# One level of Strassen's scheme for the key products of a paged attention loop

## The chip, the cores and the metric

The kernel runs on one NeuronCore of a Trainium2 chip. The metric is the device time of one execution in microseconds (us). TensorE (PE) multiplies; VectorE (DVE), ScalarE (ACT) and GpSimd (POOL) work element by element; SyncE (SP) issues nearly all DMAs. The engines run their own instruction lists in order and wait for each other on semaphores only.

## The reference

One step of a hybrid decoder layer for 256 prompt tokens and for 8 sequences ("batches" below) of 4 new tokens each. An mLSTM branch and an MLA attention branch are gated and added, then comes a convolutional feed-forward part. The change lies in the MLA attention of the 8 sequences, each of which has 1024 cached positions in 8 pages of 128 rows. A cached row is a latent of 512 numbers and a rotary key of 64:

```python
def mla_keys(c_kv, k_rope, w_uk, g_kn, g_kr):
    k_nope = jnp.einsum('...sc,chd->...shd', c_kv, w_uk)
    k_r = jnp.broadcast_to(k_rope[..., None, :], k_nope.shape[:-1] + (B_ROPE,))
    return qk_norm(k_nope, k_r, g_kn, g_kr)
def mla_attend(q, k, c_kv, mask, w_uv):
    s = jnp.einsum('bqhe,bkhe->bhqk', q, k).astype(jnp.float32) * ATTN_SCALE
    s = jnp.where(mask, s, -jnp.inf)
    p = jax.nn.softmax(s, axis=-1).astype(c_kv.dtype)
    o_lat = jnp.einsum('bhqk,bkc->bqhc', p, c_kv)
    return jnp.einsum('bqhc,chv->bqhv', o_lat, w_uv)
```

The 16 keys of 128 numbers of a cached row are needed only for their norm (qk_norm divides each key by its root mean square). The scores themselves can be had from the latent, with a query that was multiplied by w_uk beforehand.

## The kernel before

All work is in stages with barriers between them: projections and prompt attention, then the **page loop** (this change), then the mLSTM heads, branch projections, the output projection and the feed-forward part. Weights pass in tiles of 2048 columns through four staging slots (`stage`); a weight or activation is split into a high and a low part of type fp32r, and a product is made of three matmuls (high by high, high by low, low by high). `split_hi` (L281, ScalarE) and `split_lo` (L288, VectorE) split weight tiles; `block` (L300, L301, L305) multiplies one by the 288 tokens, in 48 matmuls.

**Page loop.** `batches` unrolls batches 0, 1, 6 and 7 and loops over 2 to 5, two at a time. For each page `page_load` brings the latent and rotary rows in 32 by 32 blocks, VectorE transposes them (`turn`, L1806), ScalarE rounds them to the high part (`hi`, L1707), VectorE makes the low part (`lo`, L1810). `keys` then multiplies the page (512 features in 4 chunks) by w_uk, kept in SBUF for the whole loop as `ukH` and `ukL`, in five column groups of 448, 384, 384, 384 and 512 columns, a PSUM bank each. The first group carries the 64 multiplied query columns of the batch beside three heads, so that scores come with the keys, and two small matmuls add the rotary part. ScalarE squares each group out of PSUM (`squares`, L1720), and VectorE sums the squares per head (`sums`, L1817). After eight pages `scale` turns the sums into factors on the scores. The softmax and the product with the latents (`maxima`, `spread`, `less`, `exps`, `total`, `denominators`, `values`, `turn_out`, `out`, `out_turned`) of a batch run between the pages of the next one; the latents as values are loaded a second time, untransposed (`latf`, L1488). GpSimd has nothing in this loop.

**Around it.** The stage before loads w_uk again in its last third (`uk_again`), into the four staging slots; at the loop's start four splits turn them into `ukH` and `ukL`. With that the slots are free, and SP fills them with half of w_uv and the first two weight tiles of the next stage. `ukH` and `ukL` lie where xnH and xnL (the split normed activations) lay; these are reloaded from a DRAM copy when the last key product is done (L1529, L1530). After the loop TensorE does the values of the last batch, one block of the next stage, the products with w_uv, a second block, and the stage ends.

Of the kernel before, what the change touches and what calls it, by code (L numbers as in the profile page):

```python
# [25 lines left out]
P = 128  # L26
# [144 lines left out]
def build(nc, A, O):  # L171
# [33 lines left out]
    with ctx:  # L205
# [111 lines left out]
        qlat = sb(kept, "qlat", [P, LC, NB, 2, BH, S_S], F32R)  # L317
        krr2 = sb(kept, "krr2", [P, 3, 2, ROPE])
        krr = krr2[:, :, 0, :]
        rk_new = sb(kept, "rk_new", [P, BH])  # L320
        cnH = sb(kept, "cnH", [P, LC, P], F32R)
        cnH_at = nc.sbuf_base - 4 * LC * P
        cnL = sb(kept, "cnL", [P, LC, P], F32R)
        RAW, QD = 4, P // 4
        RC = P + QD
        raw = sb(kept, "raw", [P, RAW, 4 * RC])
        raw_in = [lasting(f"raw_in{s}") for s in range(RAW)]
# [19 lines left out]
        uk_land = [lasting(f"uk_land{g}") for g in range(4)]  # L347
# [86 lines left out]
        with ExitStack() as heads:  # L434
# [39 lines left out]
            cqH, cqL = (qlat[:].rearrange("p k b o h s -> p (k b o h s)")[:, i * LC * T:(i + 1) * LC * T].rearrange("p (k t) -> p k t", k=LC) for i in range(2))  # L474
# [10 lines left out]
            def B2(name):  # L485
# [24 lines left out]
            r_t, r_sq, r_sum, r_ss, ct_t, ct_ev, cn_z = (  # L510
                sem("kr_" + x) for x in ("t", "sq", "sum", "ss", "ctt", "ctev", "cnz"))
            k_mm, k_sq, k_smp, k_sum, k_add, k_rt, k_rc, k_new, k_nadd, k_nrt = (
                sem("k_" + x) for x in ("mm", "sq", "smp", "sum", "add", "rt", "rc", "new", "nadd", "nrt"))
            u_t, u_ev, u_q, u_ab, u_abt, u_h, u_l = (sem("uk_" + x) for x in ("t", "ev", "q", "ab", "abt", "h", "l"))
# [20 lines left out]
            with nc.Block() as blk:  # L535
                @blk.sync
                def _(sp):
# [69 lines left out]
                    def uk_again(g):  # L607
                        read(VCH + g)
                        for x in range(4):
                            sp.dma_start(chunk_of(VCH + g, 512)[quadrant(x)], uk_q[x][:, :, g * 512:(g + 1) * 512]).then_inc(uk_land[g], 16)  # L610
# [4 lines left out]
                    uk_again(0)  # L615
                    uk_again(1)
# [3 lines left out]
                    for p in range(PAIRS):  # L620
                        out(p)
                        if p == 2:
                            uk_again(2)
                        if p == 4:
                            uk_again(3)

                @blk.tensor
                def _(pe):
# [147 lines left out]
                    def absorbed(j):  # L776
                        pe.wait_ge(u_ab, j + 1)
                        need(pe, u_l, LC * j)
# [124 lines left out]
                    def values(h):  # L903
                        pe.wait_ge(e_tev, h + 1)
                        pe.wait_ge(v_ev, 2 * (h // 4) + 2)
                        if h == 0:
                            pe.wait_ge(u_l, 4 * LC)
# [28 lines left out]
                def _(act):  # L936
# [120 lines left out]
                    def high_part(j):  # L1057
                        act.wait_ge(u_abt, j + 1)
                        for k in range(LC):
                            q_ = bank[7][:, k * P:(k + 1) * P].rearrange("p (g b s) -> p b g s", g=4, b=NB)  # L1060
                            act.activation(qlat[:, k, :, 0, 4 * j:4 * j + 4, :], q_, ACT.Copy).then_inc(u_h, 1)
# [112 lines left out]
                def _(dve):  # L1174
# [3 lines left out]
                    dve.memset(cnH[:].bitcast(F32), 0.0).then_inc(cn_z, 1)  # L1178
                    dve.memset(cnL[:].bitcast(F32), 0.0).then_inc(cn_z, 1)
# [112 lines left out]
                    def low_part(j):  # L1292
                        for k in range(LC):
                            q_ = bank[7][:, k * P:(k + 1) * P].rearrange("p (g b s) -> p b g s", g=4, b=NB)
                            dve.wait_ge(u_h, LC * (j + 1))
                            dve.tensor_tensor(qlat[:, k, :, 1, 4 * j:4 * j + 4, :], q_, qlat[:, k, :, 0, 4 * j:4 * j + 4, :].bitcast(F32),
                                              ALU.subtract).then_inc(u_l, 1)
                    for h in range(BH + 3):
# [16 lines left out]
                        if h >= 10 and (h - 10) % 4 == 0:  # L1315
                            low_part((h - 10) // 4)
# [31 lines left out]
                    low_part(3)  # L1348
# [21 lines left out]
        with ExitStack() as ph:  # L1370
            NJ = NPG + 1
            HQ = BH * S_S
            HALF = NPG // 2
            GC = 512
            UC = BH * NOPE + 2 * HQ
            GROUPS = [(0, 3), (3, 6), (6, 9), (9, 12), (12, 16)]
            KG = len(GROUPS)
            ukH = arena("ukH", [P, LC, UC], 0, F32R)
            ukL = arena("ukL", [P, LC, UC], 4 * LC * UC, F32R)

            def uk_col(h):

                return h * NOPE + (HQ if h < GROUPS[0][1] else 2 * HQ)

            def moving(g, s):

                h0, h1 = GROUPS[g]
                if g:
                    return uk_col(h0), uk_col(h0) + (h1 - h0) * NOPE
                return (0, h1 * NOPE + HQ) if s == 0 else (HQ, h1 * NOPE + 2 * HQ)  # L1390

            def slot(s):

                return slice(0, HQ) if s == 0 else slice(HQ + GROUPS[0][1] * NOPE, 2 * HQ + GROUPS[0][1] * NOPE)

            def parts(s):

                w = GROUPS[0][1] * NOPE
                return (slice(0, HQ), slice(HQ, HQ + w)) if s == 0 else (slice(w, w + HQ), slice(0, w))

            def key_bank(g):
                return bank[g if g < 4 else 5]

            sq = sb(ph, "sq_n", [P, 2, GC])
            mxp = sb(ph, "mxp", [P, 2, P])
            mxw = sb(ph, "mxw", [HQ, 2, P])
            sqr = sb(ph, "sqr_n", [P, 2, ROPE])
            scn = sb(ph, "scn", [N_S, NB, BH, S_S])
            latf = sb(ph, "latf", [P, 2, NPG, KVL + ROPE])
            latT = sb(ph, "latT", [P, KVL + P])  # L1410
            latH = sb(ph, "latH", [P, 2, KVL + P], F32R)
            latL = sb(ph, "latL", [P, 2, KVL], F32R)
# [4 lines left out]
            psums = sb(ph, "psums", [P, 2, HQ])  # L1417
# [1563 lines left out]
```

## Time and profile before

| | us |
|---|---|
| median of 3 runs (2891.14 to 2893.79) | 2893.04 |
| the profiled execution | 2892.51 |
| its span, first to last instruction | 2890.6 |
| TensorE busy | 2838.0 |
| VectorE busy | 1495.8 |
| ScalarE busy | 1131.8 |
| GpSimd busy | 104.6 |

The span is the time between the first and the last instruction, and the profiled execution's time is what the device took for it as a whole. "Busy" counts time in which an instruction of the engine runs; TensorE's matmuls overlap, so its busy time is no measure of how fast they follow each other.

### The profile page before, as it was taken

The page shows a single profiled execution, that of the slowest core. Times are in us where ns is not written, and L with a number is a line of the kernel's source. Part 1 is how long each engine was busy: PE and PEld are TensorE (multiplying, and loading weights), DVE is VectorE, ACT ScalarE, POOL GpSimd, SP SyncE. Part 2 cuts the span into 40 slices and gives each one's busy share as a digit, 9 for nine tenths or more (in the row PEclk, how much of TensorE's full clock was granted, in tenths as well). Part 3 has the DMA queues.
Part 4 walks back from the last instruction along what each step waited for, and adds up shares of the span by engine and source line. Part 5 has one row for each costly group of instructions (what it writes and reads, how often), then busy time and mean ns, then how long its engine had stood idle before and what let it go on. Part 6 is the DMA issues. An engine that isn't in the chain of part 4 may idle for free. (4 is left out here: it accounts for less than half of the span.)

```text
span 2890.6 us, 50971 instructions
## 1 busy us (share of the span) xinstructions
PE 2838.0 (98%) x19086; PEld 2657.2 (92%) x19086; DVE 1495.8 (52%) x2297; ACT 1131.8 (39%) x1813; POOL 104.6 (4%) x346
## 2 busy tenths in 40 slices
PE   8998999999999998999999999999999999999999
PEld 7865898898898887999999999999999999999999
DVE  5465544444444433445454434445677754677644
ACT  5536332332333232444544333333444433444433
POOL 0100000000000000000000000002100000001000
PEclk9999999999999998999999999999999999999999
DMA  6624412112212204656666555556555556555564
GB/s 196 224 77 104 132 44 58 51 37 62 58 35 53 59 31 165 188 176 191 180 195 181 161 170 165 160 171 189 163 162 160 155 157 183 168 166 161 147 176 130
DMA packets 695531, 393.32 MB, mean 136 GB/s; under 512 B 65096, under 2 KB 675986, under 8 KB 694424
## 3 DMA queue, kind: packets, MB, share of 16 engines
q1 hardware_dynamic: 683160, 378.64, 44.9%
q10 hardware_dynamic: 11824, 11.50, 1.2%
q8 instruction: 110, 1.80, 0.3%
q0 software_dynamic: 368, 0.81, 0.1%
q14 instruction: 69, 0.57, 0.1%
HBM read 368.13 MB, written 22.75 MB: 135 GB/s over the span
## 5 line engine op out<-in xcount | busy, mean ns | idle before, releaser
L288 DVE TENSOR_TENSOR w_lo_b<-stage,w_hi_b 128x2048 fp32r<-128x2048 f32 (+1 forms) x289 | 619.0, 2142 | 411.0 <-ACT w_hi_b L281 410.8
L300 PE MATMUL bank<-xnH,w_hi_b 128*128 128x288 f32 x2784 | 756.8, 299 | 3.5 <-PEq L191 3.5
L301 PE MATMUL bank<-xnL,w_hi_b 128*128 128x288 f32 x2784 | 751.4, 297 | 0.0
L281 ACT ACTIVATE w_hi_b<-stage 128x2048 fp32r<-128x2048 f32 (+1 forms) x289 | 517.8, 1792 | 568.2 <-PE bank L305 535.4
L300 PEld LDWEIGHTS bank<-xnH,w_hi_b 128*128 128x128 f32 x2784 | 524.8, 188 | 13.4 <-issue 12.8
L301 PEld LDWEIGHTS bank<-xnL,w_hi_b 128*128 128x128 f32 x2784 | 524.4, 188 | 0.3
L1556 PE MATMUL bank<-ukH,latH 128*128 128x384 f32 (+2 forms) x1280 | 458.0, 358 | 5.0 <-DVE latL L1810 3.9
L1560 PE MATMUL bank<-ukL,latH 128*128 128x384 f32 (+2 forms) x1280 | 459.7, 359 | 0.0
L1561 PE MATMUL bank<-ukH,latL 128*128 128x384 f32 (+2 forms) x1280 | 454.0, 355 | 0.0
L305 PE MATMUL bank<-xnH,w_lo_b 128*128 128x288 f32 x2784 | 396.4, 295 | 0.0
L1817 DVE TENSOR_REDUCE rk<-sq_n 128x3 f32<-128x384 f32 (+1 forms) x320 | 182.1, 574 | 403.3 <-ACT sq_n L1720 403.3
L305 PEld LDWEIGHTS bank<-xnH,w_lo_b 128*128 128x128 f32 x2784 | 378.1, 188 | 0.0
L1720 ACT ACTIVATE sq_n<-bank 128x384 f32<-128x384 f32 (+1 forms) x320 | 163.4, 511 | 437.8 <-PE bank L1561 414.2
L300 PE MATMUL bank<-haH,w_hi_b 128*128 128x288 f32 x1024 | 277.3, 298 | 6.8 <-PEq L191 3.8
L301 PE MATMUL bank<-haL,w_hi_b 128*128 128x288 f32 x1024 | 275.9, 296 | 0.0
L1556 PEld LDWEIGHTS bank<-ukH,latH 128*128 128x128 f32 x1280 | 241.2, 188 | 31.5 <-issue 12.0
L1561 PEld LDWEIGHTS bank<-ukH,latL 128*128 128x128 f32 x1280 | 241.3, 189 | 14.4
L1560 PEld LDWEIGHTS bank<-ukL,latH 128*128 128x128 f32 x1280 | 241.2, 188 | 14.1 <-issue 1.0
L300 PEld LDWEIGHTS bank<-haH,w_hi_b 128*128 128x128 f32 x1024 | 193.4, 189 | 7.5 <-issue 7.3
L301 PEld LDWEIGHTS bank<-haL,w_hi_b 128*128 128x128 f32 x1024 | 194.3, 190 | 0.0
L305 PE MATMUL bank<-haH,w_lo_b 128*128 128x288 f32 x1024 | 151.9, 295 | 0.0
L305 PEld LDWEIGHTS bank<-haH,w_lo_b 128*128 128x128 f32 x1024 | 141.6, 188 | 0.0
(480 smaller groups left out, 2757.1 us busy)
## 6 DMA issues: line engine op xcount, KB each, us to landing
stage<-in_w_in_dram SPq DMA_DIRECT2D x88, 1024.0 KB, 5.2
stage<-in_w_up_dram SPq DMA_DIRECT2D x88, 1024.0 KB, 5.4
stage<-in_w_down_dram SPq DMA_DIRECT2D x64, 704.0 KB, 4.6
raw<-in_cache_kv_latent_dram SPq DMA_DIRECT2D x256, 64.0 KB, 1.8
latf<-in_cache_kv_latent_dram SPq DMA_DIRECT2D x64, 256.0 KB, 2.5
stage<-in_w_branch_a_dram SPq DMA_DIRECT2D x16, 1024.0 KB, 5.5
stage<-in_w_branch_b_dram SPq DMA_DIRECT2D x16, 1024.0 KB, 5.3
stage<-in_w_out_dram SPq DMA_DIRECT2D x16, 1024.0 KB, 5.6
```

The source lines that it names most:

```text
L281: act.activation(h, a, ACT.Copy).then_inc(w_hi, 1)
L288: dve.tensor_tensor(lo, a, h.bitcast(F32), ALU.subtract).then_inc(w_lo, 1)
L300: pe.matmul(out, hi, xH(k), start=first and k == 0, stop=False)
L301: pe.matmul(out, hi, xL(k), start=False, stop=False)
L305: mm = pe.matmul(out, lo, xH(k), start=False, stop=last and k == kc - 1)
L1556: pe.matmul(out, h, ukH[:, k, cols], start=k == 0, stop=False)
L1560: pe.matmul(out, h, ukL[:, k, cols], start=False, stop=False)
L1561: mm = pe.matmul(out, lo, ukH[:, k, cols], start=False, stop=k == LC - 1)
L1720: act.activation(sq[:, (j + g) % 2, 0:(h1 - h0) * NOPE], part, ACT.Square).then_inc(n_sq, 1)
L1817: dve.tensor_reduce(rk[:, b.mod(2), j, h0:h1], sq[:, (j + g) % 2, 0:(h1 - h0) * NOPE].rearrange("p (h d) -> p h d", d=NOPE), AX.X, ALU.add ...
```

## The change

The pages are taken in pairs. With the features in halves 1 and 2 and the heads in halves 1 and 2, the keys of a pair are a product of two matrices of two by two blocks, A (pages by features) and B (features by heads). It is made with seven block products instead of eight (Winograd's form of Strassen's scheme):

- sums on the page side: S1 = A21 + A22, S2 = S1 - A11, S3 = A11 - A21, S4 = A12 - S2, per pair, on GpSimd; the seven operands A11, A12, S2, S3, S1, S4, A22 are split into high part (ScalarE, `split`) and low part (GpSimd, `low`)
- differences on the weight side: T1 to T4, once at the start; the seven operands B11, B21, T2, T3, T1, B22, T4 are split and stay in SBUF, also where the staging slots were
- the products p1 to p7 add up in PSUM as far as the scheme allows; ScalarE copies three partial sums out (`copy_s1`, `copy_u2`, `copy_u4`), VectorE makes three of the four results from a bank and such a copy (`sum11`, `sum22`, `sum21`), and the fourth is squared out of PSUM

Each half of the heads (8 heads) is cut into column groups of 2, 3 and 3 heads, which are 288, 384 and 384 columns wide; the first carries 32 query columns. So a pair has three groups G, twelve a batch, of seven products, and a product is two feature chunks by three matmuls, 42 matmuls a group. The products of a group are interleaved with two of the group before (p3 and p4):

```diff
-                        for j in range(NPG):
-                            keys(b, j)
+                        for G in range(NG):
+                            i, pos = G // 3, G % 3
+                            p1(b, G)
+                            p2(b, G)
+                            if pos == 0:
+                                ropes(b, i)
+                            if not early(b, G - 1):
+                                p3(b, G - 1)
+                            p6(b, G)
+                            p7(b, G)
+                            if not early(b, G - 1):
+                                p4(b, G - 1)
...
+                            p5(b, G)
```

One product, and two with their waits:

```diff
+                        for c in range(2):
+                            hi, lo = (lat[:, a, part, c * P:(c + 1) * P] for part in range(2))
+                            pe.matmul(out, hi, moving(g, op, 0, c, s), start=first and c == 0, stop=False, skip_group_check=not first)
+                            pe.matmul(out, hi, moving(g, op, 1, c, s), start=False, stop=False, skip_group_check=not first)
+                            mm = pe.matmul(out, lo, moving(g, op, 0, c, s), start=False, stop=c == 1, skip_group_check=not first)
+                        mm.then_inc(sem_, 1)
...
+                    def p6(b, G):
+                        pe.wait_ge(e_s1, upto(b, G))
+                        product(b, G, bA[G % 2], S2, T2, k_p[6], False)
...
+                    def p5(b, G):
+                        pe.wait_ge(e_u2, upto(b, G))
+                        product(b, G, bA[G % 2], S1, T1, k_p[5], False)
```

GpSimd per pair, and the order of ScalarE and VectorE in a group (without the parts for starts and ends):

```diff
+                        out, x, y, how = ((latents(S1), a21, a22, ALU.add), (latents(S2), latents(S1), a11, ALU.subtract),
+                                          (a21, a11, a21, ALU.subtract), (latents(S4), a12, latents(S2), ALU.subtract))[n]
+                        pool.tensor_tensor(out, x, y, how).then_inc(f_sum4, 1)
...
+                        pool.wait_ge(a_hi, b.of(7 * PR, 7 * i + op + 1))
+                        need(pool, a_lo, b.of(7 * PR, 7 * i + op))
+                        pool.tensor_tensor(lat[:, op, 1, :], latents(op), lat[:, op, 0, :].bitcast(F32), ALU.subtract).then_inc(a_lo, 1)
...
+                                copy_u4(b, G - 1)
+                                square(b, G - 2, C21, e_c21, e_q21)
+                                split(b, i, S1)
+                            copy_s1(b, G)
+                                split(b, i + 1, A11)
+                                square(b, G - 1, C22, e_c22, e_q22)
+                                split(b, i + 1, A12)
+                            square(b, G, C11, e_c11, e_q11)
+                                square12(b, G - 1)
+                                split(b, i, S4)
+                            copy_u2(b, G)
+                                split(b, i + 1, S2)
+                                split(b, i + 1, S3)
+                                rope_squares(b, i)
+                                    split(b, i, A22)
+                                rope_high(b, i + 1)
+                            if post and G == 2:
+                                root(b - 1)
+                            if post and G == 6:
+                                exps(b - 1)
...
+                                sum22(b, G - 1)
+                                turn(b, i + 1)
+                                norm_sum(b, G - 2, C21, 1, 0, e_q21, e_r21)
+                            sum11(b, G)
+                                norm_sum(b, G - 1, C22, 1, 1, e_q22, e_r22)
+                            norm_sum(b, G, C11, 0, 0, e_q11, e_r11)
+                                norm_sum(b, G - 1, C12, 0, 1, e_q12, e_r12)
+                                sum21(b, G - 1)
```

`turn` transposes both pages of the next pair into one buffer once a pair, when all low parts of the pair before are made. Rotary scores get four small matmuls a pair (`ropes`). The query columns of a batch are also combined and split into seven operands (`query_sums`, `query_low` on GpSimd, `query_high` on ScalarE). The softmax steps of the batch before are spread over the groups; `values` runs in groups 8 and 9, from a buffer of four pages (`value_rows`, waiting for the values' matmuls), the rotary rows have a load of their own. The scores of the new tokens are made of plain fp32 matmuls instead of split ones, and the split of the multiplied queries in the stage before is gone.

Start: `uk_again` loads w_uk by column groups into `stage`. T1 to T4 of the first and third of the groups in memory order are made by VectorE (`uk_sums`), those of the other by GpSimd; `uk_high` (ScalarE) and `uk_low` (VectorE) split the 21 operands, those of the first column group before the first product and the others in groups 0 and 1 of batch 0.

End: xnH and most of xnL are reloaded when p4 of the last pair's first group is done; the slots, the last piece of xnL and w_uv follow in this order, and the next stage's block moves ahead of the values, the second block ahead of the w_uv products:

```diff
+                    sp.wait_ge(k_p[4], upto(b, NG - 3))
+                    sp.dma_start(xnH[:].bitcast(F32), xnH_dram).then_inc(xn_back, 16)
+                    sp.dma_start(xnL[:, 0:KC - 1].bitcast(F32), xnL_dram[:, 0:KC - 1]).then_inc(xn_back, 16)
+                    sp.wait_ge(k_p[4], upto(b, NG - 2))
+                    head_load(sp, At(0), 0)
+                    uv_load(0)
                     for j in range(2, 4):
                         uv_load(j)
-                    sp.wait_ge(n_k, KG * NPG * NB)
-                    sp.dma_start(xnH[:].bitcast(F32), xnH_dram).then_inc(xn_back, 16)
-                    sp.dma_start(xnL[:].bitcast(F32), xnL_dram).then_inc(xn_back, 16)
+                    head_load(sp, At(0), 1)
+                    sp.wait_ge(k_p[4], upto(b, NG - 1))
+                    sp.dma_start(xnL[:, KC - 1:].bitcast(F32), xnL_dram[:, KC - 1:]).then_inc(xn_back, 16)
+                    uv_load(1)
                     sp.wait_ge(f_uv, 4)
```

## Rows read from the trace of the kernel before

**Rows 1.** The page, part 1: busy time, share of the span, instructions.

```profile
PE 2838.0 (98%) x19086; PEld 2657.2 (92%) x19086; DVE 1495.8 (52%) x2297; ACT 1131.8 (39%) x1813; POOL 104.6 (4%) x346
```

**Rows 2.** Stretches: start:end, length, busy time of each engine, granted clock, DMA share.

```profile
284.00:295.00 11.00, 5.71 (x19) 4.14 (x19) 6.60 (x17) 4.44 (x8) 0.00 (x0) 0.76 0.58 149
295.00:1102.00 807.00, 805.91 (x4230) 723.12 (x4230) 356.84 (x694) 259.00 (x619) 0.00 (x0) 1.00 0.21 55
1102.00:1141.00 39.00, 27.19 (x265) 20.72 (x264) 13.22 (x26) 10.26 (x14) 0.07 (x1) 0.85 0.50 183
```

**Rows 3.** Waits of TensorE, 295 to 1102: total us, times, longest.

```profile
PE bank L1556 <- DVE latL L1810: 3.9, 1, 3.9
PE bank L1556 <- issue: 1.0, 2, 0.8
```

**Rows 4.** Timeline, TensorE: start, duration; the maxima transposes of two batches.

```profile
507.60 0.27 PE L1578 MATMUL bank<-cst,mxp 128*128 128x128 f32 x1
...
608.39 0.27 PE L1578 MATMUL bank<-cst,mxp 128*128 128x128 f32 x1
```

**Rows 5.** Timeline, TensorE: first of 36 with 384 columns, first and last of 12 with 512.

```profile
701.61 0.34 PE L1556 MATMUL bank<-ukH,latH 128*128 128x384 f32 x1
...
707.86 0.39 PE L1556 MATMUL bank<-ukH,latH 128*128 128x512 f32 x1
...
710.42 0.39 PE L1561 MATMUL bank<-ukH,latL 128*128 128x512 f32 x1
```

**Rows 6.** Timeline, TensorE: third of 12 with 448 columns, and the one after the last.

```profile
711.40 0.37 PE L1561 MATMUL bank<-ukH,latL 128*128 128x448 f32 x1
...
713.44 0.34 PE L1556 MATMUL bank<-ukH,latH 128*128 128x384 f32 x1
```

**Rows 7.** Timeline, TensorE: first matmuls of two neighbouring projection blocks, 48 apart.

```profile
1149.69 0.29 PE L300 MATMUL bank<-xnH,w_hi_b 128*128 128x288 f32 x1
...
1156.09 0.29 PE L300 MATMUL bank<-xnH,w_hi_b 128*128 128x288 f32 x1
```

**Rows 8.** Groups by shape, 400 to 1100, weight loads: count, busy us, mean ns, idle before.

```profile
L1560 PEld LDWEIGHTS bank<-ukL,latH 128*128 128x128 f32 x1109 | 208.5, 188 | 12.2 <-issue 1.0
```

**Rows 9.** The same view, ScalarE.

```profile
L1720 ACT ACTIVATE sq_n<-bank 128x384 f32<-128x384 f32 x223 | 109.1, 490 | 255.0 <-PE bank L1561 239.2 <-DVE rk L1817 14.8 <-issue 0.9
...
L1707 ACT ACTIVATE latH<-latT 128x640 fp32r<-128x640 f32 x54 | 39.2, 726 | 0.0
...
L1729 ACT ACT_TABLE_LOAD x7 | 9.0, 1283 | 0.1
```

**Rows 10.** The same view, VectorE.

```profile
L1817 DVE TENSOR_REDUCE rk<-sq_n 128x3 f32<-128x384 f32 x223 | 120.7, 547 | 228.7 <-ACT sq_n L1720 228.7
...
L1806 DVE STREAM_TRANSPOSE latT<-raw 128x640 f32<-128x640 f32 x54 | 45.6, 845 | 7.2
...
L1831 DVE RECIPROCAL rk<-rk 128x128 f32<-128x128 f32 x6 | 5.7, 953 | 4.2 <-ACT rk L1724 4.2
...
L1854 DVE TENSOR_TENSOR sc_s<-sc_s,bank 128x512 f32<-128x512 f32 x7 | 4.7, 677 | 0.0
```

**Rows 11.** Groups by shape, whole span, GpSimd.

```profile
L2852 POOL TENSOR_TENSOR sqs<-sqs 128x288 f32<-128x288 f32 x15 | 31.0, 2065 | 68.8 <-ACT sqs L2769 68.8
...
L2268 POOL TENSOR_TENSOR qm<-qT_m,cst 128x256 f32<-128x256 f32 x8 | 5.1, 638 | 1052.0 <-ACT qT_m L2187 941.0 <-PE bank L2141 110.9
```

**Rows 12.** Timeline, GpSimd, in the output projection.

```profile
1942.36 2.15 POOL L2852 TENSOR_TENSOR sqs<-sqs 128x288 f32<-128x288 f32 x1 [4.38 <-ACT sqs L2769]
```

**Rows 13.** Timeline, VectorE, at the same time.

```profile
1941.56 2.29 DVE L288 TENSOR_TENSOR w_lo_b<-stage,w_hi_b 128x2048 fp32r<-128x2048 f32 x1 [1.55 <-ACT w_hi_b L281]
```

**Rows 14.** DMA issues: size, median us from issue to landing.

```profile
xnL<-xnL_scratch SPq DMA_DIRECT2D x1, 2304.0 KB, 13.8
```

**Rows 15.** Timeline, TensorE: the first block after the loop.

```profile
1118.12 0.40 PE L300 MATMUL bank<-xnH,w_hi_b 128*128 128x288 f32 x1
```

More of the change, by code:

```diff
@@ L346, in build @@
         page_in, uv_in = lasting("page_in"), lasting("uv_in")
[L347 removed]
+        uk_land = [lasting(f"uk_land{g}") for g in range(3)]
         e_st = [lasting("e_st0"), lasting("e_st1")]
@@ L1392, in slot @@
[L1392 to L1406, printed above, removed]
+            PR = NPG // 2
@@ L1467, in batches, with page_rows @@
+                return stage[:, (3, 0)[j - 2], :].rearrange("p (k m) -> p k m", k=LC)
+            def page_rows(b, j, last):
+                if last and j >= 4:
+                    return raw[:, j % RAW, 0:KVL]
+                return vals[:, j % 4, :]
             def batches(body):
@@ L1506, in _, with batch @@
-                    for j in range(NPG):
-                        load(At(0), j)
+                    def batch(b, post, last):
+                        for i in range(PR):
+                            if not last or i == 0:
+                                ahead(b, i + 3)
+                            if post and i == 1:
+                                for j in range(4):
+                                    value_rows(b - 1, j)
+                            if post and i == 2:
+                                for j in range(4, NPG):
+                                    value_rows(b - 1, j)
@@ L1508, in _ @@
+                    for j in range(4):
+                        rope_rows(At(0), j)
+                    ahead(At(0), 2)
                     sp.dma_start(gb[:], A["b_gates"].broadcast_to([P, 2 * AH])).then_inc(g_in, 16)
@@ new lines, in p5, with ropes @@
+                    def p5(b, G):
+                        pe.wait_ge(e_u2, upto(b, G))
+                        product(b, G, bA[G % 2], S1, T1, k_p[5], False)
+                    def ropes(b, i):
+                        pe.wait_ge(f_rl, pairs(b, i))
+                        need(pe, e_rope, pairs(b, i - 1))
+                        for x in range(2):
+                            out = bR[:, (2 * (i % 2) + x) * HQ:(2 * (i % 2) + x + 1) * HQ]
+                            pe.matmul(out, rope[:, x, :], qHH[:, bass.ds(b.of(), 1), :], start=True, stop=False)
+                            mm = pe.matmul(out, rope[:, x, :], qLZ[:, bass.ds(b.of(), 1), :], start=False, stop=True)
+                        mm.then_inc(k_rope, 1)
```

906 lines of the change are left out of this document (618 added, 288 removed).

## Prediction

> **What bounds the kernel now.** I read four views in this order: the engine line of the page, the table of stretches, TensorE's waits in the page loop, and the start times of single matmuls there. The engine line shows TensorE busy for 98% of the span, VectorE 52%, ScalarE 39%, GpSimd 4% [rows 1]. The table of stretches shows where this change acts. The page loop runs from 295 to 1102, 807 us, with TensorE busy throughout, VectorE 357, ScalarE 259, and GpSimd nothing; 11 us lie ahead of it and 39 us behind it in which TensorE has holes [rows 2]. Inside the loop TensorE waited 4.9 us in all [rows 3]. So the loop lasts as long as its matmuls do, and only what changes their number or their spacing moves the end, as long as the three other engines keep up.
>
> A matmul's own duration is no price here, since neighbours overlap; the spacing of starts is. 36 matmuls of 384 columns take from 701.61 to 707.86, 173.6 ns each, and 11 of 512 take 2.56 us, 232.7 ns [rows 5]. Ten of 448 take 2.04 us, 204 ns [rows 6]. Of 288 columns there is none in the loop, but a projection block of the next stage has 48 in 6.40 us, 133.3 ns [rows 7]. A batch of eight pages is the distance of two maxima transposes: 100.8 us [rows 4].
>
> **The products removed.** Before, a page is 12 matmuls in each of five column groups (448, three of 384, 512): 12 x (204 + 3 x 173.6 + 232.7) ns = 11.49 us, so a pair is 22.98 us. After, a pair is three groups (288, 384, 384 columns) of seven products of six matmuls: 42 x (133.3 + 2 x 173.6) ns = 20.18 us. That is 2.80 us a pair, 89.6 us over 32 pairs. Rope products, values, transposes and denominators stay on TensorE as they are (the rest of the 100.8 us, about 9 us a batch), so a batch would become 89.6 us and a pair 22.4 on average. The columns fall by exactly an eighth, the matmuls do not (126 for 120 a pair), and the gain still comes out at 12.2%, since the spacing at 288 columns is cheap.
>
> Each of these matmuls has its own weight load of 188 ns [rows 8], yet starts stand 173.6 and even 133.3 ns apart, so loads overlap and the loads don't set the spacing. The Trainium skill (Perfetto Trace Analysis, Identifying the Most-Contended Engine) says to judge TensorE's headroom by the busy share of its weight loads; by that rule the loop is loaded to 90% and six more loads a pair at 188 ns would add 36 us over 32 pairs. The spacing of rows 7 contradicts that rule here.
>
> **What ScalarE and VectorE get.** Before, ScalarE squares and VectorE reduces five tiles a page, ten a pair. After, each of the three groups of a pair has three copies out of PSUM and four squares on ScalarE, and three sums and four reductions on VectorE. ScalarE: 384 columns cost 0.49 us and a 640-column copy 0.73 [rows 9], so a 256-column split is about 0.37. A pair is 21 such passes, those of the first group shorter (about 9.4 us), seven splits (2.6), the rope copy and squares (1.2): 13 us of 22.4. VectorE: a reduction is 0.55, an add of PSUM and SBUF is 0.68 at 512 columns, so about 0.54 at 384, a page transpose 0.85, the reciprocal of the batch 0.95 [rows 10]; 21 x 0.5 + 1.7 + about 1.5 of scores and rope, and some 7 us a batch of softmax, make about 15.5 us a pair. Both stay under TensorE's 22.4, so they cost only where one comes late for a partial sum that TensorE waits for.
>
> I walk one 384-column group (a product is 1.04 us, a group 7.3). The copy after the first product ends near 1.75 us, and TensorE needs it at 2.9 to 3.1. The copy of the second partial sum (after p6) ends near 5.1, wanted at 6.0 to 6.2. The last copy of a group ends 0.7 us into the next one, wanted at 2. The slack is about 1 us each time, so ordinary groups cost nothing. Two groups of a batch are worse: ScalarE changes its table for the square root and for the exponential, 1.28 us each [rows 9], at the end of a group, and VectorE stands behind the root with its reciprocal (0.95) and product (0.69) before the last sum of the group. After the root, the copy that TensorE needs is ready 3.6 us into the next group and wanted at 2.8; after the exponential, similar. I take 1.5 us a batch, seven batches: +10 us (bounds 0 and 4 us a batch, 28). The same table loads were covered before by whole column groups of slack.
>
> **GpSimd** had nothing to do in the loop; now it makes four sums and seven low parts a pair, 256 columns each, and the split queries once a batch. Its nearest row is 638 ns for a product of 256 columns; the other end is 2065 ns for 288 columns [rows 11]. The second is not the operation: GpSimd's add began at 1942.36 and lasted 2.15 us, and VectorE had a 2.29 us subtraction of two SBUF operands running from 1941.56 [rows 12, 13]; it ended at 1943.85, and 0.65 us after that the add was done. I take 0.64, for in the loop VectorE's long instructions read PSUM or a single SBUF tile; the two-SBUF ones are short. 11 x 0.64 = 7 us a pair, a third of TensorE's time. The Trainium skill (SBUF — State Buffer, Who interferes with whom) says the two share a port pair as an exclusive lock, taken by a VectorE instruction with two SBUF inputs; rows 12 and 13 agree, 1.5 us of blocking.
>
> **Start of the loop.** Before, four large splits of the key matrix run in a row, and TensorE waited 3.9 us for the first page [rows 3]. After, seven operands for each of three column groups are formed, partly by differences, and split, in step with the first groups. For the second and third group that is 7 x 768 columns on ScalarE (0.8 each) and on VectorE (0.95 each), plus four differences: the first three groups of the first batch need about 30 us where their matmuls take 18. GpSimd's sums of that stretch and VectorE's two-SBUF subtractions exclude each other as in rows 12 and 13, which adds several us more. I take +15 (bounds +4 and +22). The compressed new-token scores there (plain fp32 rather than three split products) and VectorE's dropped low parts of the stage before are at most 1 us; hidden behind these chains.
>
> **End of the loop.** Before, the reload of xnH and xnL (4.7 MB) was issued at the last key product and landed 13.8 us later [rows 14]; the first projection block began at 1118.1 [rows 15], 16 us after the last product. Staging slots were filled long before. After, the reload starts some 11 us earlier, but SP now issues behind it the two head tiles and three of the four w_uv pieces (5 MB), because their slots held key operands, and the last piece of xnL lies behind these. 10 MB at the 342 GB/s of rows 14 is 29 us, landing 18 us after the last product: +2. Then the second block stands ahead of the w_uv products, and the next head tiles are issued only after these, so 6.4 us of cover for them is gone. Part of the wait also falls at TensorE's lower clock, as now (granted 0.85 in this stretch, rows 2). I take +10 (bounds +3 and +18).
>
> SP's other work per page is the same ten transfers; page rows for the values are now loaded four at a time behind the values' matmuls. DMA is 21% busy in the loop [rows 2] and a group of 7 us lies between their release and use, so nothing.
>
> **Sum.** -89.6 + 10 + 15 + 10 = -54.6 us. The profiled execution took 2892.5 us (span 2890.6), half a microsecond under the median of 2893.0, so about 2838.
>
> **Rivals.** (a) The partial-sum chains don't keep their slack: semaphores and queues on ScalarE (about a dozen instructions a group) cost 0.3 to 0.5 us more each, and every group stalls about 0.4 us: 96 x 0.4 = 38 us, 2876. For it: two-way handovers of one accumulator with 1 us slack. Against it: two squares back to back stand closer than their durations, and TensorE shows no bubble at group boundaries before.
> (b) GpSimd becomes the bound, and the kernel slower. The transposed pages have one buffer, so the transposes (2.9 us with their wait) and all 11 GpSimd operations follow in a ring: 2.9 + 11 x per pair. It passes TensorE's 22.4 at x = 1.77 us, and the old kernel's pair (25.2, less 0.8 for start and end) at about 1.95. At 2.07, the mean of rows 11, the pair is 25.7: 32 x 0.5 + 25 = +41, 2933. It needs each operation to meet a VectorE lock, which rows 12 and 13 show only beside 2.29 us subtractions.
> (c) The change doesn't shorten TensorE's work, since weight loads pace it (the rule above): 2893 + 36 + 25 = 2954. Rows 7 speak against it.
> (d) Start and end hide fully and no stall comes: 2893 - 89.6 + 7 = 2810.
>
> **Chances.** Forecast 0.62 (2820 to 2858), (a) 0.18, (d) 0.09, (b) 0.09, (c) 0.02. The range that holds 8 in 10 runs from 2808 to 2882. What can be told from no change is about 0.2%, 6 us: faster 0.88, same 0.02 (a part of (b) near its point of balance), slower 0.10.
>
> **What would show it.** A batch in the loop near 91 us by two maxima transposes; matmul starts 173 and 133 ns apart; TensorE waits in the loop of some 10 us, on ScalarE's copies after root and exponential; ScalarE near 60% and VectorE near 70% busy there, GpSimd near a third with 0.64 us operations. The first group's start near 291 and steady groups only from about 325; the first projection block 18 us behind the last key product. Wrong if GpSimd operations exceed 1.7 us, if waits repeat in every group, or if 288-column starts stand 170 ns apart.

## The result, and the profile after

The changed kernel takes 2895.66 us (median of 19 runs, 2894.18 to 2901.59), the kernel before in the same comparison 2891.3. The ratio is 1.0015, 95% interval 1.0009 to 1.0022: slower by 0.15%. Forecast were 2838 us and a gain. The profiled execution took 2897.9 us, its span is 2895.7, 5.1 more than before. The forecast gain of the matmuls arrived; the rest of this text is about what ate it.

The page of the changed kernel, part 1, and its table of stretches (start:end, length, busy time of PE, PEld, DVE, ACT and POOL, granted clock, DMA share, GB/s), against [rows 1, 2]:

```profile
PE 2779.4 (96%) x19274; PEld 2622.9 (91%) x19274; DVE 1629.0 (56%) x2705; ACT 1300.4 (45%) x2332; POOL 403.6 (14%) x763
...
284.00:295.00 11.00, 8.73 (x24) 3.02 (x25) 8.52 (x14) 3.74 (x12) 7.53 (x11) 0.69 0.18 43
295.00:1094.00 799.00, 744.10 (x4415) 687.73 (x4414) 491.73 (x1119) 426.74 (x1134) 289.14 (x406) 0.97 0.20 55
1094.00:1146.00 52.00, 29.18 (x262) 24.33 (x263) 13.47 (x30) 11.60 (x15) 0.04 (x1) 0.77 0.49 167
```

Over the whole span TensorE is 59 us less busy, yet its loop is only 8 us shorter (799 for 807): it now has 55 us of holes, where it had 1. The end grew from 39 to 52 us.

Timeline of TensorE in the changed kernel, against [rows 5, 7]: a product of 384 columns, its first and fourth matmul, and the start of the next product of 288 columns.

```profile
711.84 0.34 PE L1649 MATMUL bank<-uk_all,lat 128*128 128x384 f32 x1
...
712.36 0.34 PE L1649 MATMUL bank<-uk_all,lat 128*128 128x384 f32 x1
...
712.88 0.29 PE L1649 MATMUL bank<-uk_all,lat 128*128 128x288 f32 x1
713.01 0.30 PE L1650 MATMUL bank<-uk_all,lat 128*128 128x288 f32 x1
713.14 0.30 PE L1651 MATMUL bank<-uk_all,lat 128*128 128x288 f32 x1
```

Six matmuls of 384 columns in 1.04 us are 173 ns each, and those of 288 stand 130 to 135 ns apart: the price of the sum was right. Their weight loads take 188 ns as before:

```profile
L1651 PEld LDWEIGHTS bank<-uk_all,lat 128*128 128x128 f32 x1138 | 213.9, 188 | 0.0
```

But a batch, by two maxima transposes against [rows 4], takes 98.2 us, where 100.8 were before and about 91 forecast:

```profile
836.11 0.27 PE L1706 MATMUL bank<-cst,mxp 128*128 128x128 f32 x1
...
934.34 0.27 PE L1706 MATMUL bank<-cst,mxp 128*128 128x128 f32 x1
```

TensorE's waits between 280 and 1110 in the changed kernel (total us, times, longest) name what stands in between, against [rows 3]:

```profile
PE bank L1761 <- DMA vals<-in_cache_kv_latent_dram: 24.5, 7, 4.5
PE bank L1649 <- ACT su L1853: 15.6, 8, 12.0
PE bank L1649 <- ACT su L1847: 9.8, 8, 6.5
PE bank L300 <- issue: 8.2, 1, 8.2
```

The largest was forecast at nothing: the values product waits for its rows. Of the waits on ScalarE's copies two are long ones at the start (12.0 and 6.5); what is left of these two rows is 6.9, where 10 were forecast. The last row is the first block after the loop.

SyncE's timeline around one values product (x4: four transfers together; the duration is that of issuing), then ScalarE's and TensorE's there:

```profile
651.91 1.46 SPq L1564 DMA_DIRECT2D rows_r<-in_cache_k_rope_dram  x2
654.26 4.01 SPq L1578 DMA_DIRECT2D vals<-in_cache_kv_latent_dram  x4
...
668.16 0.38 SPq L357 DMA_DIRECT2D raw<-in_cache_k_rope_dram  x1
675.50 1.47 SPq L1564 DMA_DIRECT2D rows_r<-in_cache_k_rope_dram  x2
677.86 3.82 SPq L1578 DMA_DIRECT2D vals<-in_cache_kv_latent_dram  x4
```

```profile
675.37 0.19 ACT L1896 ACTIVATION_READ_ACCUMULATOR sqr_n<-rows_r 128x1 f32 x1
```

```profile
667.60 1.92 PE L1761 MATMUL bank<-vals,sc_s 128*64 128x512 f32 x8
...
680.71 2.27 PE L1761 MATMUL bank<-vals,sc_s 128*64 128x512 f32 x3 [4.22 <-DMA vals<-in_cache_kv_latent_dram]
```

The first half of the values product is over at 669.5, and with it the four buffers are free. The second four rows are issued only at 677.9, right behind two rotary rows. These go to the next batch's second page pair, and wait for `f_ss`, the count of ScalarE's squares of the rotary rows that fill their buffers now, those of this batch's last pair. SyncE reaches the load at 668.5; the squares are done at 675.5, a whole group later. SyncE takes its list in order, so the value rows wait too. TensorE then waits 4.2 us, and 3.3 us again inside the product while the later rows come: 7.5 us in each of batches 1 to 6. The last batch loads no rotary rows for a next one and has no such wait.

### The profile page after: what moved, and what is told of

The parts are those of the page before. It is cut to its first block and busy times, and to the rows that moved or that the text cites. A ratio compares the mean times of both kernels' runs of the same rounds, so it can differ in the third digit from the quotient of the medians.

```text
span 2895.7 us, 54132 instructions
## 1 busy us (share of the span) xinstructions
PE 2779.4 (96%) x19274; PEld 2622.9 (91%) x19274; DVE 1629.0 (56%) x2705; ACT 1300.4 (45%) x2332; POOL 403.6 (14%) x763
## 5 line engine op out<-in xcount | busy, mean ns | idle before, releaser
L1649 PE MATMUL bank<-uk_all,lat 128*128 128x384 f32 (+1 forms) x1280 | 424.2, 331 | 29.1 <-ACT su L1853 15.6
L1651 PE MATMUL bank<-uk_all,lat 128*128 128x384 f32 (+1 forms) x1280 | 414.4, 324 | 0.0
L1650 PE MATMUL bank<-uk_all,lat 128*128 128x384 f32 (+1 forms) x960 | 306.7, 319 | 0.0
L1649 PEld LDWEIGHTS bank<-uk_all,lat 128*128 128x128 f32 x1280 | 242.6, 190 | 50.3 <-issue 19.2
L1651 PEld LDWEIGHTS bank<-uk_all,lat 128*128 128x128 f32 x1280 | 242.5, 189 | 0.0
L2169 DVE TENSOR_REDUCE rk<-cb 128x3 f32<-128x384 f32 (+1 forms) x384 | 185.6, 499 | 16.3 <-ACT cb L1864 5.5
L1864 ACT ACTIVATE cb<-cb 128x384 f32<-128x384 f32 (+1 forms) x288 | 139.6, 485 | 102.0 <-DVE cb L2147 74.7
L1650 PEld LDWEIGHTS bank<-uk_all,lat 128*128 128x128 f32 x960 | 182.8, 190 | 0.0
L2049 POOL TENSOR_TENSOR lat<-latT,lat 128x256 fp32r<-128x256 f32 x160 | 118.8, 743 | 228.5 <-ACT lat L1882 158.2
```

Of the source, the lines that this page charges most:

```text
L1649: pe.matmul(out, hi, moving(g, op, 0, c, s), start=first and c == 0, stop=False, skip_group_check=not first)
L1650: pe.matmul(out, hi, moving(g, op, 1, c, s), start=False, stop=False, skip_group_check=not first)
L1651: mm = pe.matmul(out, lo, moving(g, op, 0, c, s), start=False, stop=c == 1, skip_group_check=not first)
L1864: act.activation(x[:, p_], x[:, p_], ACT.Square).then_inc(done, 1)
L2049: pool.tensor_tensor(lat[:, op, 1, :], latents(op), lat[:, op, 0, :].bitcast(F32), ALU.subtract).then_inc(a_lo, 1)
L2169: ins = dve.tensor_reduce(rk[:, s, 2 * (G // 3) + page_, half * BH // 2 + h0:half * BH // 2 + h1], x[:, key_part(g, s)].rearrange("p (h d) ...
```

## Experiments

Each was timed beside the kernel before (2890.3 to 2892.2 in these comparisons). "Against the changed kernel" is the difference of the ratios, with that of the spans of the two profiled executions beside it.

**1. Value rows ahead of the rotary rows.** SyncE issues rows 4 to 7 of the values first.

```diff
-                                ahead(b, i + 3)
+                                ahead(b, i + 3, not (post and i == 2))
...
                                 for j in range(4, NPG):
                                     value_rows(b - 1, j)
+                                if not last:
+                                    rope_rows(b + 1, 2)
+                                    rope_rows(b + 1, 3)
```

> Only SP's order is changed: value rows 4 to 7 of the batch before are issued ahead of the two rotary rows of the next batch, which wait for ScalarE. Theory A (in-order queue: in the changed kernel the value rows stood behind that wait, and TensorE lost about 7.5 us in each of six batches, 4.2 before the second half of the values and 3.3 within it): the maxima transposes come 90 to 92 us apart instead of 98, the time falls by 40 to 47 us, to about 2850, and no wait of TensorE on the value rows is left. Rival B (the rows are late because transfers are slow beside the page loads): the order changes nothing, 98 us a batch and 2895.

Measured: 2852.02 us (2849.62 to 2854.89), ratio 0.9856 [0.9840, 0.9873], so 1.6% or 46 us less than the changed kernel; span 2852.7, 43.0 less. The wait on the values is gone, and a batch is 91.0 us:

```profile
533.79 0.27 PE L1710 MATMUL bank<-cst,mxp 128*128 128x128 f32 x1
624.76 0.27 PE L1710 MATMUL bank<-cst,mxp 128*128 128x128 f32 x1
```

This order alone decides between faster and slower.

**2. The same wait taken away in another way.** The order stays; rotary rows of page pairs 1 and 3 (counted from 0) get buffers of their own, so that the load has nothing to wait for. Two small buffers of the gate computation move into spare memory to make room.

```diff
-            rows_r = sb(ph, "rows_r", [P, 4, ROPE])
+            rows_r = sb(ph, "rows_r", [P, 6, ROPE])
+            rslot = (0, 1, 2, 3, 0, 1, 4, 5)
...
-                        need(sp, f_ss, b.of(NPG, j + 1 - 4))
+                        need(sp, f_ss, b.of(NPG, j + 1 - (4 if rslot[j] < 2 else NPG)))
```

> The changed kernel with SyncE's order as it is, but the rotary rows of page pairs 1 and 3 of a batch in buffers of their own (6 row buffers for 4), so that the load of the next batch's pair 1 has nothing to wait for; the value rows stay behind it. (Two small buffers of the gate computation move into spare memory for room.) Theory A (the value rows are late because they stand in SyncE's in-order queue behind a load that waits for ScalarE's squares of the rotary rows): the same -40 to -47 us as moving them ahead, about 2853, and no wait of TensorE on the values in the middle batches. Theory B (what the first edit changed was the place of some 18 transfers among each other, that is the time SyncE or the DMA engines need for them): with the order kept, 0 to -10 us, 2886 to 2896.

Measured: 2856.36 (2852.62 to 2859.55), ratio 0.9887 [0.9872, 0.9902], 37 us less; span 2850.4, 45.3 less. SyncE's timeline at the same place, from the last page load on:

```profile
652.25 0.38 SPq L357 DMA_DIRECT2D raw<-in_cache_k_rope_dram  x1
653.39 1.46 SPq L1565 DMA_DIRECT2D rows_r<-in_cache_k_rope_dram  x2
655.74 3.82 SPq L1579 DMA_DIRECT2D vals<-in_cache_kv_latent_dram  x4
```

The rotary rows follow the page load at once, and no wait on the values is left. So it was the waiting load ahead of them, and not the number or place of the transfers. The median is some 4 us above that of experiment 1, the span 2 below; this difference stays open.

**3. The lock at the start.** VectorE makes the differences of the middle column group in place of GpSimd.

```diff
-                    pool.tensor_tensor(t1, b12, b11, ALU.subtract).then_inc(uk_sumY, 1)
...
+                            dve.tensor_tensor(out_, x, y, ALU.subtract).then_inc(uk_sumY, 1)
...
                             if start and G == 1:
+                                uk_sums_y()
```

> The four differences of the second column group in memory order move from GpSimd to VectorE, ahead of that group's low parts. Theory A (VectorE and GpSimd exclude each other when VectorE reads two SBUF tiles: its four differences of 768 columns took 2.44 us each beside GpSimd's): they take 0.95 us each, 6 us less, VectorE gets 3.8 us more to do a group later, and the first three groups end 2 to 6 us earlier; the whole 2 to 6 us less than the changed kernel. Rival B (768 columns simply take 2.44 us on VectorE): eight such differences in a row, the start 6 to 10 us later.

Measured: 2894.63, ratio 1.0010 [1.0000, 1.0020], 1.4 us less; span 2892.2, 3.5 less. VectorE's differences at the start, first in the changed kernel, where GpSimd makes its own at that time, then in this one:

```profile
303.34 2.58 DVE L2287 TENSOR_TENSOR uk_all_f<-stage 128x768 f32<-128x768 f32 x1
305.96 2.44 DVE L2287 TENSOR_TENSOR uk_all_f<-stage,uk_all_f 128x768 f32<-128x768 f32 x1
```

```profile
305.19 2.39 POOL L2125 TENSOR_TENSOR uk_more_f<-stage,uk_more_f 128x768 f32<-128x768 f32 x1
```

```profile
303.27 0.96 DVE L2275 TENSOR_TENSOR uk_all_f<-stage,uk_all_f 128x768 f32<-128x768 f32 x1
```

The blocking is real, 2.44 for 0.96 us, and four instructions lost 6 us by it. Yet VectorE then has the other four to make, 5.1 us, and nearly all of it goes there.

**4. Differences earlier.** VectorE makes those of the second column group before the low parts of the first, where it had gaps.

```diff
-                                uk_sums(1)
...
                     rope_low(At(0), 0)
+                    uk_sums(1)
                     for x in range(2, 7):
```

(ScalarE's first copy of a partial sum moves up as well.)

> Order of the start only: VectorE's differences for the second column group are made in its idle time before the low parts of the first group are done, and ScalarE's first copy of a partial sum comes in the middle of the splits. Theory A (TensorE's waits of 6.5 and 12.0 us there come from the order: the copy for p5 stood behind a square, that behind VectorE's first sum, that behind four differences and two low parts): the two waits shrink to some 5 us together, the time is 8 to 14 us under the changed kernel's. Rival B (the start is bound by the amount of splitting on VectorE and GpSimd): the waits move to the next group, 0 to 3 us less.

Measured: 2892.94, ratio 1.0001 [0.9991, 1.0011], 4.0 us less; span 2889.1, 6.6 less. The wait of 12.0 is 9.1, and one of 5.1 on VectorE's low parts is new. The forecast of 8 to 14 was too high.

**5. The end of the loop, two edits.** SyncE issues the last piece of xnL ahead of the w_uv pieces and the second head tile; and the w_uv products stand ahead of the second block again.

```diff
                     head_load(sp, At(0), 0)
-                    uv_load(0)
-                    for j in range(2, 4):
-                        uv_load(j)
-                    head_load(sp, At(0), 1)
                     sp.wait_ge(k_p[4], upto(b, NG - 1))
                     sp.dma_start(xnL[:, KC - 1:].bitcast(F32), xnL_dram[:, KC - 1:]).then_inc(xn_back, 16)
-                    uv_load(1)
+                    for j in range(4):
+                        uv_load(j)
+                    head_load(sp, At(0), 1)
...
-                    first_block(N0 + 1)
                     pe.wait_ge(uv_in, 16 * LC)
...
                         mm.then_inc(f_uv, 1)
+                    first_block(N0 + 1)
```

> End of the loop only: the last piece of xnL is issued ahead of w_uv and of the second head tile, and the w_uv products come before the second block again. Theory A (TensorE's 8.2 us wait before the first block is for a piece of xnL queued behind 4 MB, and the 8 us before the next stage are the head tiles issued after the w_uv products): the first block begins near 1102 instead of 1109 and the next stage some 10 us earlier; 9 to 14 us less. Rival B (the DMA engines are full in that stretch, 10 MB have to pass whatever the order): the wait turns up ahead of the w_uv products instead, under 4 us less.

Measured: 2885.49, ratio 0.9978 [0.9968, 0.9988], 10.7 us less; span 2883.3, 12.4 less.

**6. The first of the two alone.**

> The changed kernel with one half of the edit at the end: SyncE issues the last piece of xnL ahead of the w_uv pieces and the second head tile; the w_uv products stay behind the second block. Theory A (two losses of their own: the first block starts 8 us late behind that piece, and the head tiles come late since the slots are released 6.4 us later by the moved block): the first block starts 8 us earlier, and of the 11 us of both edits 6 to 9 come: 2886 to 2890. Theory B (the end waits for the head tiles alone, which only the order of the w_uv products sets): the first block starts earlier, but the next stage does not: 0 to -2 us.

Measured: 2891.07, ratio 0.9995 [0.9985, 1.0004], 5.8 us less; span 2888.4, 7.3 less. The first block, and the first of the next stage, in the changed kernel, with one edit (6) and with both (5), one fence each:

```profile
1109.07 0.58 PE L300 MATMUL bank<-xnH,w_hi_b 128*128 128x288 f32 x1 [8.18 <-issue]
...
1145.65 0.58 PE L300 MATMUL bank<-xnH,w_hi_b 128*128 128x288 f32 x1 [7.67 <-PEq L191]
```

```profile
1100.28 0.61 PE L300 MATMUL bank<-xnH,w_hi_b 128*128 128x288 f32 x1
...
1137.79 0.58 PE L300 MATMUL bank<-xnH,w_hi_b 128*128 128x288 f32 x1 [7.66 <-PEq L191]
```

```profile
1101.11 0.61 PE L300 MATMUL bank<-xnH,w_hi_b 128*128 128x288 f32 x1
...
1134.83 0.37 PE L300 MATMUL bank<-xnH,w_hi_b 128*128 128x288 f32 x1 [3.75 <-PEq L191]
```

And in the kernel before, the last matmul of the loop and the first block of the next stage:

```profile
1101.88 0.40 PE L1561 MATMUL bank<-ukH,latL 128*128 128x512 f32 x1
...
1140.61 0.58 PE L300 MATMUL bank<-xnH,w_hi_b 128*128 128x288 f32 x1 [3.51 <-PEq L191]
```

In the three kernels the last key product ends at 1093.1, 1092.6 and 1093.4. From there to the next stage are 52.6, 45.2 and 41.4 us: 7.4 for the piece of xnL that stood behind the other loads, 3.8 for the block ahead of the w_uv products (the wait before the next stage falls from 7.7 to 3.75). 41.4 is 3 us over the 38.3 of before.

**7. All four (1, 3, 4, 5).**

> All four edits together: the value rows 4 to 7 ahead of the rotary rows in SyncE's queue, the differences of the middle column group on VectorE, VectorE's other differences ahead of the idle time at the start, and the last piece of xnL ahead of the w_uv pieces with the w_uv products ahead of the second block. Theory A (four separate places, each loss paid on its own): against the changed kernel (2895.7) about -43.6 for the value rows, -11 for the end, and for the start more than the -3 and -5 of the two edits alone, since the differences then run at 0.95 us and in time that VectorE had idle: -10; together -64, about 2831 (2826 to 2838), faster than both kernels. Theory B (the places share one cause further up, or what one edit gives back the next stage takes): less than -50, above 2845.

Measured: 2838.23 us (2835.35 to 2839.08), ratio 0.9818 [0.9804, 0.9831]; span 2836.6, 59.1 less than the changed kernel. The spans of the four edits alone add up to 65.5 less, so nearly all of it adds up (Theory A, with 59 for its 64, at the upper edge of its range). This version beats the kernel before by 1.8%.

**8. The start once more.** On top of 7, VectorE's differences one by one between the low parts, ScalarE's second copy in groups 0 and 1 ahead of splits and squares, and the first sum of group 1 ahead of the middle group's differences.

```diff
                     for x in range(2, 7):
                         uk_low(0, x)
+                        if x < 6:
+                            uk_sums(1, (x - 2,))
...
                             copy_s1(b, G)
+                            if start and G == 0:
+                                copy_u2(b, G)
```

> The kernel with all four edits, and the start once more: VectorE's differences for the second column group one by one between the low parts of the first (in the gaps of 1.6 us in which it waited for ScalarE) instead of in one piece ahead of them; in groups 0 and 1 of batch 0, ScalarE copies the second partial sum before it splits key operands and before it waits for a square; VectorE makes the first sum of group 1 ahead of the differences of the middle column group. Theory A (TensorE's three waits at the start, 5.0, 5.9 and 6.3 us, are only the order of short instructions on ScalarE and VectorE): 8 to 14 us less than the 2838 of the four edits, 2824 to 2830. Theory B (VectorE and ScalarE are simply full there, and what one group gains the next waits for): 0 to -3 us.

Measured: 2839.43 us (2836.0 to 2840.0), ratio 0.9816 [0.9803, 0.9829]; span 2837.4. No gain: Theory B. TensorE's waits at the start, first with the four edits, then here:

```profile
299.96 0.58 PE L1651 MATMUL bank<-uk_all,lat 128*128 128x288 f32 x1 [4.97 <-DVE uk_all L2297]
309.07 0.61 PE L1651 MATMUL bank<-uk_all,lat 128*128 128x288 f32 x1 [5.89 <-ACT su L1855]
324.63 0.69 PE L1651 MATMUL bank<-uk_all,lat 128*128 128x384 f32 x1 [6.32 <-ACT su L1855]
```

```profile
302.21 0.61 PE L1651 MATMUL bank<-uk_all,lat 128*128 128x288 f32 x1 [2.27 <-ACT su L1855]
...
324.74 0.66 PE L1651 MATMUL bank<-uk_all,lat 128*128 128x384 f32 x1 [6.39 <-DVE sc_s L2177]
```

The waits of 5.0 and 5.9 became several of 1.2 to 2.3, and the third ended at the same moment, 324.7 for 324.6. The first maxima transpose stands at 437.4 for 437.3. Between 304 and 327 VectorE's timeline of this kernel shows one gap, of 0.7 us, so VectorE is full there. That its work now sets the length of the start fits this, but no run lessened that work.

**9. More work for GpSimd.** On top of 1, each low part is made twice.

```diff
+                        for m in range(2):
+                            ins = pool.tensor_tensor(lat[:, op, 1, :], latents(op), lat[:, op, 0, :].bitcast(F32), ALU.subtract)
+                            if m < 1:
+                                ins.then_inc(x_lo, 1)
+                                pool.wait_ge(x_lo, b.of(7 * PR * 1, (7 * i + op) * 1 + m + 1))
+                        ins.then_inc(a_lo, 1)
```

> The kernel with the value rows moved ahead (2852 us), and each of GpSimd's low parts made twice into the same place, 18 operations a pair for 11. Theory A (GpSimd's work counts only by the ring of transposes and its operations, 2.9 + 18 x 0.74 = 16.2 us a pair, under TensorE's 20.5): no change, 2850 to 2856. Theory B (GpSimd's and VectorE's two-operand instructions exclude each other, so more GpSimd work makes VectorE's sums late that TensorE waits for): 224 more operations, each costing VectorE some of its 0.74 us, and ScalarE's and VectorE's chains with 1 us of slack: +10 us or more, from 2862.

Measured: 2860.53 (2859.03 to 2862.19), ratio 0.9899 [0.9884, 0.9914], 12 us over experiment 1; span 2857.3, 4.6 over. A steady batch is 91.2 us (538.16 to 629.32) for 91.0. The long waits at the start are 13.1 and 10.6 us for 12.0 and 6.6 in experiment 1. The first maxima transpose stands at 447.0 for 442.8, so 4.2 of the 4.6 us fall at the start; by what, no run shows. In the loop VectorE's sums that TensorE waits for take what they took (550 to 556 ns at 384 columns for 549 to 557); only its short additions of 32 columns are longer, 295 ns for 187. The trace doesn't show all of the 12 us, so for the total the run is inconclusive between the two theories.

**10. Four times.** As before, with four of each.

> The same with each low part made four times, 32 operations a pair. Theory A (the ring of 2.9 + 32 x 0.74 = 26.6 us a pair now passes TensorE's, four pairs are 106 us for the batch's 91): +15.4 us a batch, about 2975 (2945 to 3000, lower if the transposes overlap GpSimd). Theory B (the lock): much above 3000.

Measured: 3164.69 us in one run; span 3162.5. A batch is 129.6 us (five take 647.8, by maxima transposes at 502.4 and 1150.2). TensorE's waits in the loop, and GpSimd's main groups in one batch (502.5 to 631.8):

```profile
PE bank L1654 <- POOL lat L2055: 132.1, 97, 2.3
PE bank L1654 <- ACT su L1858: 69.5, 31, 8.8
```

```profile
L2055 POOL TENSOR_TENSOR lat<-latT,lat 128x256 fp32r<-128x256 f32 x80 | 59.6, 745 | 21.2 <-issue 11.4 <-ACT lat L1887 2.9
L2055 POOL TENSOR_TENSOR lat<-sT,lat 128x256 fp32r<-128x256 f32 x32 | 23.4, 732 | 2.8 <-POOL latT L2046 0.2
...
L2046 POOL TENSOR_TENSOR sT<-latT 128x256 f32<-128x256 f32 x4 | 2.9, 730 | 5.4 <-DVE latT L2210 5.3
```

The time lies far above Theory A's range, where Theory B put it, yet not for its reason: the operations are hardly longer than in the changed kernel (745 and 732 ns for 738 and 732), so no lock makes them slow. The ring was mis-drawn: a pair takes 32.4 us, of which 32 operations are 23.8, and 8.6, not 2.9, lie between them (transposes, issue, waits for splits, and 0.8 of query operations). With that constant rival (b) would set in near (22.4 - 8.6) / 11 = 1.3 us an operation, not 1.77. This is an estimate, and rather low, since the gaps between the repeated operations are in the 8.6.

## Why the prediction was wrong, step by step

- **Products, -89.6 with stalls +10: right.** Experiment 1 shows a batch of 91.0 us, as forecast, 9.8 less than before; over eight batches -78.4, against -79.6 forecast for both terms. Stalls on ScalarE's copies were 0.7 us a batch in the steady loop (the forecast had 1.5). Rivals (a) and (c) are refuted by the same batch.
- **The step that failed: "DMA is 21% busy in the loop [rows 2] and a group of 7 us lies between their release and use, so nothing."** The share of DMA and the time after the release were both right, and neither was the question. The text on SyncE did not ask what is queued ahead of the value rows: a load that waits for ScalarE's squares, which are made a group later. The rows left 8.4 us after their buffers were free. This cost 43 to 46 us (experiment 1; 37 to 45 by experiment 2), more than half of the products' gain, and turned a gain into a loss.
- **Start, +15 (bounds 4 to 22): too low.** In experiment 1 the loop takes 755.4 us (294.7 to 1050.1); less eight batches of 91.0 that is 27.4, where before had 0.8. So +27. 20.3 us are TensorE's waits there on ScalarE's copies; most of the rest goes with its clock, granted at 0.76 between 295 and 345 and at 1.00 in the 50 us after. The 12 us of splits beyond the matmuls were seen, and so was the blocking of [rows 12, 13], put at "several us": it took 6 on VectorE alone, where both engines make differences out of SBUF at the same time. But taking it away gave back only 1.4 us, or 3.5 by the spans (experiment 3), so it explains little of the 12 us missed. The rest is not taken apart: experiments 4 and 8 point to the amount of VectorE's work there, which no run lessened. The Trainium skill (SBUF — State Buffer, SBUF: two separate sides) says of a VectorE instruction with two SBUF inputs and a GpSimd one that reads SBUF that whichever starts first has the shared ports for the whole instruction; the 2.44 us for 0.96 agree.
- **End, +10 (bounds 3 to 18): within its bounds, +14.** The first block came 16.0 us behind the last product, 18 were forecast, 16 before. That wait was the same length, but before, the values of the last batch filled its second half (1110.95 to 1118), and now they follow the block, at 1118.4. The step looked only at when the block could start and not at what stood in the hole before it. Of the 14.2, 7.4 go back to the last piece of xnL, sent behind 5 MB of other loads (experiment 6 moves it ahead of four of them, 1 MB each), and 3.8 to the late head tiles, where 8 were implied; 3 are left.
- **GpSimd, 0.64 us an operation, off the path: right in effect.** It was 0.74, and GpSimd was 39% busy in a steady batch. The ring's constant was too small by up to a factor of three (experiment 10), without consequence at 11 operations.

Sum of the parts: -78.4 (products with stalls) + 26.6 (start) + 14.2 (end) + 44 (value rows, 7.3 in six batches) = +6.4. The span shows +5.1; the difference is the loop's first matmul, which comes at 293.8 for 295.05. With the one failed step at zero the same parts give -38, as experiment 1 does (span 2852.7, 37.9 below before; the 26.6 was read from it, so this is a check of the end and not of the start). That is inside the forecast's range, 17 us short of its middle, 12 of them at the start and 4 at the end.

## What to carry to other kernels

For every DMA that a change moves behind a new release, read what stands ahead of it in its issuing queue and what each of those waits for: time between release and use, and the share of DMA, say nothing about that. A gain that is spread over a loop can be eaten by a single late load per iteration, and both a reordering and a deeper buffer of the load ahead give it back. When operands are made in step with their first use, add up each engine's work over that whole stretch: once one engine is full, better order moves the waits and not the end.

## What the runs showed of the hardware

- Issuing was not free while the DMA engines were busy. At the end of the changed kernel's loop single issues of SyncE took microseconds, with 379 to 417 GB/s moving between 1085 and 1110 (issues of SyncE, start and duration):

```profile
1088.67 6.04 SPq L1586 DMA_DIRECT2D uk_more_f<-in_w_uv_dram  x1
...
1097.03 8.27 SPq L1629 DMA_DIRECT2D xnL<-xnL_scratch  x1
```

The last piece of xnL was reached at 1097.0, 4 us after the last product, and landed 11.8 us later. In experiment 6, ahead of four of the loads, its issue began at 1092.6, took 1.6 us, and it landed after 5.1. So the order of loads was an order in time beyond what their semaphores asked for.
- GpSimd's subtraction of 256 columns took 732 to 745 ns in the mean however many of them ran, 11 a pair with VectorE 64% busy or 32 a pair; it stretched beside VectorE's long two-SBUF instructions at the start (up to 1.3 us). VectorE lost 1.5 us on a 0.96 us instruction there.
